# Three half turns of an expert stream, placed earlier in a fused inference step

## The reference

```
xn = rmsnorm(x) ; [qA kA vA | qB kB vB | f | gA gB] = xn @ w_in
yA = chunk-band attention(qA, kA, vA, relative bias), 8 heads of 128
yB = forgetting attention(qB, kB, vB, cumulative log sigmoid(f)), 8 heads
m  = sigmoid(gA) * (yA @ w_br_a) + sigmoid(gB) * (yB @ w_br_b)
h  = x + m @ w_out
q  = rmsnorm(h) @ w_pq ; top 16 of 128 keys per half, top 16 of 256 sums, per head
y  = h + sum over 8*16 experts e:  gate_e * gelu(u_e . rmsnorm(h)) * v_e
```

## Time and profile before

| | us |
|---|---|
| median of 3 runs | 2883.03 |
| lowest, highest | 2875.1, 2890.59 |
| profiled execution, whole | 2896.63 |
| its span | 2893.8 |
| busy in the span: TensorE | 2116.6 (73%) |
| VectorE | 1919.8 (66%) |
| GpSimd | 1262.9 (44%) |
| ScalarE | 473.4 (16%) |
| DMA, mean | 362 GB/s, 1047.10 MB |

### The profile page before, as it was taken

How to read it: one execution, slowest core, us unless ns; L and a number is a source line. 1 busy time by engine, 2 the same in 40 slices (tenths; PEclk the granted TensorE clock), 3 DMA queues, 4 the chain that set the end, 5 groups by cost and what they waited for, 6 DMA issues and landing times.

```text
span 2893.8 us, 19574 instructions
## 1 busy us (share of the span) xinstructions
PE 2116.6 (73%) x6070; PEld 1069.9 (37%) x6070; DVE 1919.8 (66%) x2669; ACT 473.4 (16%) x1107; POOL 1262.9 (44%) x854
## 2 busy tenths in 40 slices
PE   7999999999999898878999900000331038999997
PEld 3665544444545443333444400000231025444443
DVE  1122000397687756756675999999999998666666
ACT  1222100112222211001001100000894034000000
POOL 2000000024354445434453267666688865444444
PEclk9999999999999999999999955555555557999998
DMA  9777688989999989999999999999899998999999
GB/s 355 275 281 258 218 284 298 307 308 402 357 394 399 396 343 412 411 361 412 408 409 364 392 342 369 371 371 376 332 405 421 422 352 266 409 404 410 409 408 360
DMA packets 271464, 1047.10 MB, mean 362 GB/s; under 512 B 19856, under 2 KB 19856, under 8 KB 203280
## 3 DMA queue, kind: packets, MB, share of 16 engines
q0 software_dynamic: 113792, 697.85, 60.8%
q1 hardware_dynamic: 154880, 343.97, 32.8%
q10 hardware_dynamic: 2704, 4.21, 0.4%
HBM read 1036.50 MB, written 9.45 MB: 361 GB/s over the span
## 4 chain that ended last, share of the span: by engine, by line
PE 38%; DMA 24%; DVE 22%; POOL 8%; issue 6%; ACT 1%; SPq 0%; DVEq 0%; POOLq 0%; ACTq 0%
PE ps L583 34%; DMA yTr<-in_peer_v,fold 13%; DVE bigs L1571 7%; POOL bigr L554 6%; DMA bigr<-in_w_in 3%; DVE bigr L1571 3%; DVE hr L1601 3%; DMA bigr<-in_w_br_a 3%; DMA bigs<-in_peer_v,idxnow 2%; DVE spare L1571 2%; POOL spare L554 1%; DVE pwork L1386 1%; DMA bigr<-in_w_out 1%; PE ps L644 1%; DMA bigs<-in_peer_u,idxnow 1%
## 5 line engine op out<-in xcount | busy, mean ns | idle before, releaser
L583 PE MATMUL ps<-bigr 128*128 128x512 f32 x1920 | 861.9, 607 | 37.6 <-DMA bigr<-in_w_in 22.4
L583 PEld LDWEIGHTS ps<-bigr 128*128 128x128 f32 x1920 | 368.9, 195 | 490.6 <-issue 441.8
L507 POOL DMA_INDIRECT bigs<-in_peer_u,idxnow x128 | 235.7, 1841 | 547.1 <-DVE bigs L1516 526.9
L583 PE MATMUL ps<-bigr,bigs 128*128 128x512 f32 x896 | 407.4, 609 | 23.3 <-DMA bigr<-in_w_in 19.6
L1601 DVE SCALAR_TENSOR_TENSOR hr<-yTr,fold,hr 128x1024 f32<-128x1024 f32 x205 | 263.0, 1283 | 142.6 <-DMA yTr<-in_peer_v,fold 141.8
L1506 DVE SCALAR_TENSOR_TENSOR bigs<-bigs,acts 128x2048 f32<-128x2048 f32 x128 | 300.7, 2349 | 63.8 <-DMA bigs<-in_peer_v,idxnow 63.7
L1516 DVE SCALAR_TENSOR_TENSOR bigs<-bigs 128x2048 f32<-128x2048 f32 x128 | 292.9, 2289 | 66.4 <-DMA bigs<-in_peer_u,idxnow 65.2
L564 POOL DMA_INDIRECT yTr<-in_peer_v,fold x205 | 210.1, 1025 | 230.7 <-DVE hr L1601 220.4
L1571 DVE SCALAR_TENSOR_TENSOR bigr<-bigr 128x2048 f32<-128x2048 f32 x122 | 278.1, 2290 | 14.9 <-DMA bigr<-in_peer_u,fold 14.2
L848 PE MATMUL ps<-ident,fold 128*128 128x128 f32 x2 | 0.9, 472 | 386.1 <-DVE fold L1577 386.1
L554 POOL DMA_INDIRECT bigr<-in_peer_u,fold x122 | 253.0, 2074 | 66.5 <-issue 34.3
(11 more groups left out here) (257 smaller groups left out, 2254.9 us busy)
## 6 DMA issues: line engine op xcount, KB each, us to landing
bigr<-in_w_in SPq DMA_DIRECT2D x160, 1024.0 KB, 9.6
spare<-in_peer_v SPq DMA_DIRECT2D x96, 512.0 KB, 6.7
bigr<-in_w_out SPq DMA_DIRECT2D x32, 1024.0 KB, 8.8
bigr<-in_w_pq SPq DMA_DIRECT2D x32, 1024.0 KB, 7.8
bigr<-in_w_br_a SPq DMA_DIRECT2D x16, 1024.0 KB, 10.1
bigr<-in_w_br_b SPq DMA_DIRECT2D x16, 1024.0 KB, 9.9
bigr<-in_peer_v SPq DMA_DIRECT2D x32, 512.0 KB, 6.7
bigr<-in_ckT_a POOLq DMA_DIRECT2D x2, 2048.0 KB, 10.2
```

The source lines that it names most:

```text
L507: pool.indirect_dma_start(row, None, table[:, :], bass.IndirectOffsetOnAxis(ap=col, axis=0)).then_inc(loaded, 16)
L583: last = mm(ps[:, bank + t, :], src[:, k0 + k, t * P:(t + 1) * P], wring[:, s, k, :], start=(k0 + k == 0), stop=(k0 + k == kt - 1))
```

## The change

Two tables of half turns change, in the programs of VectorE and ScalarE alike. The group with index 1 gets two half turns after its query norm where it had one. Gate pass 0 gets three ahead of its first product where it had one. Passes 1, 2 and 3 get one after the mix where they had two. The stream has 64 half turns as before; the constants serve S as well, but S's own pass runs without half turns.

```
-HALVES = ((2, 1, 2, 1, 1), (1, 1, 2, 1, 1), (1, 1, 2, 1, 1), (1, 2, 2, 1, 0))
+HALVES = ((2, 1, 2, 1, 1), (2, 1, 2, 1, 1), (1, 1, 2, 1, 1), (1, 2, 2, 1, 0))
 PICK_HALVES = (0, 1, 1, 0)
-PASS_HALVES = ((1, 1, 2), (4, 1, 2), (4, 1, 2), (4, 1, 2))
+PASS_HALVES = ((3, 1, 2), (4, 1, 1), (4, 1, 1), (4, 1, 1))
 OUT_HALVES = (2, 2, 2, 2)
 QUERY_HALVES = (2, 2, 0, 0)
```

## The result

The kernel after takes 2893.81 us (median of 20 runs, 2888.61 to 2901.12), the kernel before 2888.16 us (20 runs, 2874.45 to 2903.72). The ratio is 1.0026, 95% interval 1.0013 to 1.0038: between 4 and 11 us slower. The profiled execution took 2897.78 us, its span is 2895.6.

What follows compares the result with a forecast made beforehand. The prediction took the changed stretch as bound by DMA bytes, with holes, and by TensorE in the holes. Terms +3 +6 +9 -8 +0 -8 gave +2 us on 2883, so 2885 us, range 2866 to 2900.

Steps and rivals of the forecast that it cites:

- The second group (+3): Group with index 1: its added half turn nearly fits the DMA hole, ending 2.3 us late; +3 us, bounds 0 and +10.2.
- pass 0 (+6): Gate pass 0: two added half turns make the first product 6.1 us late; +6 us, bounds 0 and +11.
- the pace of a full DMA: While gathers and weights share full DMA engines, one half turn's rows take 12.9 us; used for second group and pass 0.
- The parity step: Second group to pass 3: one more half turn shifts which begin a turn, so passes 1 to 3 have no gelu wait.
- Pass 1 (+9): Gate pass 1: six half turns before its first product as before, but no gelu wait; +9 us, bounds 0 and +12.
- Pass 2 (-8): Gate pass 2: five half turns ahead of the first product shorten it to 104.6 us; -8 us, bounds -20.6 and -5.
- Pass 3 (0): Gate pass 3: stays 104.6 us, its sixth half turn having cost TensorE nothing; 0 us, bounds -12.8 and +2.
- the output stage (-8): Output stage: one half turn less behind the mix relieves full DMA; -8 us, bounds -4 and -10.2.
- Rival A: Second group and passes: holes are filled and none opens, weights getting through; -17 us, about 2866 us; chance 0.22.
- Rival B: Pass 0: wait before first branch product decides, mix 10 us or more late; +15 us, about 2898 us; chance 0.18.

Runs made afterwards that it cites:

- e3: Kernel before with gelus of three instead of two of four half turns behind the first sigmoid in passes 1 to 3; 2892.57 us, ratio 1.0013 to kernel before.
- e2: Kernel before with only pass 0's two half turns added, one less behind the mixes of passes 2 and 3; 2893.81 us, ratio 1.0027 to kernel before.
- e4: Kernel after with all four half turns' gelus behind the second sigmoid in passes 1 to 3; 2898.61 us, ratio 1.004 to kernel before.
- e9: e6 with one half turn of passes 1 to 3 moved from ahead of the first product to between the products; 2884.03 us, ratio 0.9999 to kernel before.
- e5: Kernel after with the second group's added half turn moved behind the mix of pass 3; 2878.59 us, ratio 0.9993 to kernel before.
- e8: e6 with gelus of three of the four half turns behind the first sigmoid in passes 1 to 3; 2872.22 us, ratio 0.9946 to kernel before.
- e10: e8 unchanged, timed again in five rounds; 2871.42 us, ratio 0.9941 to kernel before.
- e1: Kernel before with only the second group's half turn added and one taken from behind pass 3's mix; 2891.02 us, ratio 1.0007 to kernel before.
- e6: Kernel after with one half turn moved from pass 0 to behind the mix of pass 3; 2874.06 us, ratio 0.9965 to kernel before.
- e7: e6 with one half turn moved from behind pass 3 to behind the output stage's second norm; 2887.8 us, ratio 1.001 to kernel before.

## Why the prediction was right, and where it was off

The forecast was +2 us and no change that can be told; it is +5.7 by the medians and +7.5 by the ratio. The small size was right. But the change can be told from none: the prediction took 0.5% as what a measurement resolves, and the 20 runs of each kernel resolved 0.26%. By its steps:

- The second group (+3) and pass 0 (+6) came at +1.8 and +6.6. In the second group two errors offset each other in part: the key norm came 4.9 us later against the query norm (31.1 us behind it, before 26.2), not 1 to 3, and 3 us of that were caught up behind it, where the gelu wait of 3.93 us was gone. The first product of pass 0 stood at 1078.01, 23.9 us behind the first branch piece, against 17.0 before: +6.9 for the 6.1 worked out from a half turn at the pace of a full DMA. That pace, 12.9 us, was the number that carried the step.
- The parity step was right. It is shown by e3, which lengthened passes 1 and 3 by 7 to 9 us each by taking a wait away, and e2, in which the same pass 0 as after was followed by a pass 1 of 101.6 us, odd. Over all profiles but those of e4 and e9, whose order is another, the nine passes of seven half turns with the wait at the second sigmoid took 100.2 to 105.4 us, and the twelve without it 103.6 to 116.2; only pass 2 of e3 is below 106. Even passes of six half turns were 99.1 to 103.5 us in the kernel after and in e2; odd ones were 88.4 to 97.2 in e5 to e8 and e10, most of them 91 to 93.
- Pass 1 (+9) was the term that was mis-sized: +15.7 and +11.5, mean +13.6. I took the even pass 2 before, +11.9, and then took 3 us off because weights had been further ahead in pass 1. Just before I had written that pass 0 leaves the ring less full, and that was the right sentence: TensorE had three pieces in pass 1 without a wait, not seven. e1 separates the two. Its pass 1 is even behind a light pass 0 and takes 106.8 us, so by this one profile the parity is worth about 6 us and the full DMA of pass 0, once parity is even, another 5 to 9.
- Pass 2 (-8) came at -9.8, the reading that five half turns end some 63 us behind the mix. Pass 3 (0) came at -2.4 and the output stage (-8) at -7.3, both with a scatter of 4 to 6 us between profiles.
- Rival A fell: the holes were filled, and passes 1 and 2 opened new ones (DMA share 0.92 to 0.97). Rival B fell by its own condition, a mix of pass 0 that is 10 us late or more: it was 6 to 7. But its pass 1, +12, was nearer to the measured +13.6 than the forecast's +9, and the time of +7.5 lies about halfway between the forecast's +2 and B's +15.
- There is luck in the sum. Pass 1 was 4.6 us worse than its term, and the other terms together 4.2 us better than theirs, so that the stages of the four profiles add up to +2.4, as if every term had been right.

What the terms left out is how stages are tied. A hole at the end of a pass is not lost whole, since the next starts with more of its weights there (pass 2 and the output stage in e3, the output stage in e8). And the prediction took the waits as they fell, where moving one half turn more put one into every pass and made the kernel faster than the one after by 18 us (e6) and 23 us (e8). By the profiles 6 to 7 us of that are pass 0, which is short again; the passes behind it are 28 to 34 us shorter in e6, and the output stage gives 13 of them back.

The rest of the difference between +2 and +7.5 isn't resolved by stage: the two pairs of profiles give +6.5 and -2.0. Nor is its cause shown. Of the two parts of the change, e2 has pass 0's alone and is as slow as the kernel after, and e1 has the second group's alone and can't be told from the kernel before; so, as far as the whole time tells, it goes with pass 0.

## What to carry to other kernels

Where a stream of large gathers and a stream of weights share full DMA engines, count in which order each is asked for. Here, as long as gathers were outstanding, the weights got as many packets as they did and so a fifth of the bytes, and TensorE starved. A wait of 3 to 10 us that held the gathers back ahead of the point where the weights were due was worth more than it cost; one of 21 to 26 us (e4) was not. When half turns are moved by an odd number, look at what else flips with them, before counting bytes: the kernel after lost its waits that way, and e7 got one of 13 us.

## What the runs showed of the hardware

With both queues filled, the gathers' queue and the weights' queue moved the same number of packets in a stretch, 2767 and 2769, although a packet of the one was 7.3 KB and one of the other 2.0 KB. So the shares of the bytes were 79% and 21%, and weight pieces of 1 MiB came 11.7 to 12 us apart while rows were outstanding. With VectorE waiting and fewer rows asked for, the weights got 951 packets to 303 (e6), and a piece took about 5.5 us. The Trainium skill ("DMA: Bandwidth & Descriptors", section "Queues, rings and completion order") has each DMA engine go round robin between its queues a packet at a time. The equal counts agree with that, as far as the packets that the profile counts are those, which no run here shows. Stages of one kernel scattered by up to 6 us between two profiles.
